# A shortened opening, one product for the spread rows, earlier evictions and a gather that comes out turned

## The reference

```python
h = concat(meta, x_prompt)                      # 272 rows, and 8 samples beside them
u = rmsnorm(h, norm_mix) @ w_in                 # 1024 -> 4640 columns
xc = silu(causal_conv(xa)); q, k = xc @ w_q, xc @ w_k; v = xa @ w_v      # per head, 128 x 128
h_a = mlstm_chunk_scan(q, k, v, ig, fg)         # states C (128 x 128 per head and sample), n, m
y   = ssd_chunk_scan(silu(causal_conv(xbc)), dt, A)
h = h + concat(gated h_a, gated y) @ w_out
xn = rmsnorm(h, norm_ffn)                       # meta rows dropped: 256 + 8 tokens
group = top1(xn @ w_r1); experts = top2(xn @ w_r2 in that group)
h = h + sum_e gate_e * (silu(xn @ w_gate[e]) * (xn @ w_up[e])) @ w_down[e]
return rmsnorm(h, norm_final), the prompt's states, the samples' states
```

## Time and profile before

| | us |
|---|---|
| runs (three) | 786.55, 788.24, 788.31; median 788.24 |
| the profiled execution | 787.24, its span 785.4 |
| PE busy | 752.2 (96%) |
| DVE, ACT busy | 276.8 (35%), 219.8 (28%) |
| bytes moved | 263.68 MB, mean 336 GB/s |

### The profile page before, as it was taken

One profiled execution on the slowest core, in us unless ns is written; L12 is line 12 of the kernel. 1 busy time (PEld: TensorE's weight loads), 2 busy tenths in 40 slices (PEclk: granted clock), 3 DMA queues, 4 the chain that ended last, 5 costly groups with the idle time before them and its releaser, 6 DMA issues.

```text
span 785.4 us, 9604 instructions
## 1 busy us (share of the span) xinstructions
PE 752.2 (96%) x3789; PEld 403.0 (51%) x3789; DVE 276.8 (35%) x657; ACT 219.8 (28%) x630; POOL 30.1 (4%) x89
## 2 busy tenths in 40 slices
PE   6997999998999999999999999999999999999995
PEld 5876888876788887533333333333333333332232
DVE  4934565768877311430030131121210201311204
ACT  4226666738765101611100101001011011001003
POOL 6100000001000100000000000000000000000000
PEclk9999999999999999999999999999999999999998
DMA  9954377965895687779999999999999999999992
GB/s 259 326 187 127 117 227 235 319 217 168 278 310 178 260 331 311 283 275 431 426 428 429 426 427 426 428 426 427 428 425 428 427 426 428 424 428 427 426 399 79
DMA packets 76347, 263.68 MB, mean 336 GB/s; under 512 B 7382, under 2 KB 46554, under 8 KB 62840
## 3 DMA queue, kind: packets, MB, share of 16 engines
q1 hardware_dynamic: 74512, 259.02, 84.4%
q0 software_dynamic: 1568, 3.91, 1.4%
q10 hardware_dynamic: 216, 0.07, 0.0%
HBM read 251.15 MB, written 11.99 MB: 335 GB/s over the span
## 4 chain that ended last, share of the span: by engine, by line
PE 81%; DMA 6%; DVE 6%; ACT 4%; issue 1%; POOL 1%; DVEq 0%; POOLq 0%; ACTq 0%
PE bank L2331 26%; PE bank L2410 12%; PE bank L1908 10%; PE bank L2181 7%; DMA arena<-in_w_down 6%; PE bank L2290 4%; PE bank L1896 4%; PE bank L2356 4%; PE bank L1995 2%; ACT h_tok L1006 1%; DVE h_tok L1442 1%; PE bank L2300 1%; PE bank L2344 1%; DVE xn L1392 1%; PE bank L2309 1%
## 5 line engine op out<-in xcount | busy, mean ns | idle before, releaser
L2331 PE MATMUL bank<-ring,arena 128*64 128x512 f32 x640 | 144.5, 596 | 4.7 <-DMA ring<-in_w_up 2.5
L1908 PE MATMUL bank<-arena,ring 128*128 128x264 f32 (+1 forms) x448 | 109.6, 400 | 4.4 <-ACT xn L928 1.7
L1908 PEld LDWEIGHTS bank<-arena,ring 128*128 128x128 f32 x448 | 84.9, 193 | 21.1 <-issue 2.8
L2331 PEld LDWEIGHTS bank<-ring,arena 128*64 128x64 f32 x640 | 43.5, 137 | 92.6 <-issue 83.1
L513 DVE COPY arena<-bank 64x512 f32<-64x512 f32 x15 | 10.2, 683 | 203.9 <-PE bank L2410 203.9
L2410 PE MATMUL bank<-ring,arena 128*64 128x512 f32 x272 | 60.5, 593 | 1.9 <-DMA ring<-in_w_down 1.9
L1773 DVE TENSOR_TENSOR arena<-bank,WG 128x512 f32<-128x512 f32 x16 | 16.9, 1055 | 126.4 <-PE bank L2331 126.4
L2181 PE MATMUL bank<-arena,ring 128*128 128x264 f32 x256 | 58.4, 387 | 0.0
L2331 PE MATMUL bank<-arena 128*64 128x512 f32 x240 | 54.6, 597 | 0.0
L2181 PEld LDWEIGHTS bank<-arena,ring 128*128 128x128 f32 x256 | 48.3, 190 | 8.5 <-issue 0.3
L1237 ACT ACTIVATE arena<-bank 128x512 f32<-128x512 f32 x15 | 9.0, 597 | 144.7 <-PE bank L2344 144.7
(11 more groups left out here) (401 smaller groups left out, 836.6 us busy)
## 6 DMA issues: line engine op xcount, KB each, us to landing
ring<-in_w_gate SPq DMA_DIRECT2D x20, 2048.0 KB, 26.0
ring<-in_w_up SPq DMA_DIRECT2D x20, 2048.0 KB, 28.5
ring<-in_w_down SPq DMA_DIRECT2D x17, 2048.0 KB, 26.8
ring<-in_w_in SPq DMA_DIRECT2D x9, 2048.0 KB, 10.8
arena<-in_w_down SPq DMA_DIRECT2D x7, 2048.0 KB, 29.4
arena<-in_w_up SPq DMA_DIRECT2D x6, 2048.0 KB, 22.1
arena<-in_w_gate SPq DMA_DIRECT2D x6, 2048.0 KB, 31.8
out<-h_tok SPq DMA_DIRECT2D x16, 512.0 KB, 3.8
```

What stands on the lines that cost most here:

```text
L1908: last = mm(b[:, q0:T], slot_k(UNIT_SLOT[u], 512)[:, k, o:o + P], hT[:, k, q0:T], start=(k == 0), stop=(k == KD - 1))
L2331: last = mm(b[CAP * half:CAP * (half + 1), :], XG[:, k, (e % 2) * CAP:(e % 2 + 1) * CAP], w(kk)[:, half * 512:(half + 1) * 512], start=(k ...
```

## The change

- **Opening.** `ident` is made first on POOL and signals at once; PE starts on extra transposes of `ident` (`turning`, 14, then 8, 6 and 4 between the real ones). ACT's table load stands ahead of its DMA issues. ACT, not DVE, normalises the small tile, and PE transposes the parameters behind tile 0's normalised rows and the second `turning`. POOL's writes of p_m, s_m and xt_dram now come ahead of the router's loads, and so the latter wait for `rows_pre`.
- **Spread rows.** DVE forms RS and RX times a diagonal (RSD, RXD: three multiplications), and PE spreads them with one product of 128 columns and two of 136, in `rows_turned`, which stands behind the seventh tile, ahead of the eighth. `row_exps` moves ahead by one eviction.
- **Evictions.** The samples' values get a signal of their own and are copied by ACT ahead of the wait for `tm_ready`; the first conv tile of head 0 is evicted ahead of `decay_state(1)`.
- **Gather.** xn is the stationary operand and PX moves with 128 columns, so the result is turned already; `rows_out`, `turn` and GT go. It stands at the head of the loop for expert 2p-1.
- **End.** The gain products go ahead, behind expert 15's first projection, into banks 0 and 1; `last_down` uses banks 2 and 3; the third tile of `last_scatter(0)` (8 rows) moves behind `last_down(1)`. DVE's order there is as it was.

```diff
+            link(g.memset(ident[:], 0.0))
+            g.affine_select(out=ident[:], in_=ident[:], compare_op=ALU.not_equal, fill=1.0, base=0, ...).then_inc(s.consts, 1)
...
+            turning(14, 7)
             for i in range(2):
                 pe.wait_ge(x_in[i], 16)
...
+                if i == 0:
+                    turning(8, 7)
...
+            turning(6, 7)
+            pe.wait_ge(s.xn_ready, 2)
             pe.wait_ge(s.params_in, 16 * 8)
...
-            normalised(2, NB + META)
+            dve.wait_ge(s.h_std, 3)
+            v.reciprocal(st3[0:NB + META, 6:7], st3[0:NB + META, 6:7]).then_inc(s.pv_ready, 1)
...
+            def rows_turned():
+                pe.wait_ge(s.rows_exp, 2)
...
+                mm(bank[5][:, 0:HA * 16], ones[0:HA, :], RSD, start=True, stop=True)
+                for j in range(2):
+                    mm(bank[5][j * HD:(j + 1) * HD, P:P + KD * 17], ones[0:HB, 0:HD], RXD[j], start=True, stop=True)
...
+                if n0_ == 6:
+                    rows_turned()
...
-            for h in range(HA):
-                mm(bank[5][:, h * 16:(h + 1) * 16], col(ident[0:HA, :], h), RS[:, :], start=True, stop=True)
-            for c in range(KD):
-                for j in range(2):
-                    last = mm(bank[5][j * HD:(j + 1) * HD, 128 + c * 17:128 + (c + 1) * 17], ...)
...
+                    if h == 0:
+                        evac(HA + XBC_A[h])
                     decay_state(h + 1)
-                    evac(HA + XBC_A[h])
...
-                def gather(p, half, tiles, done=False):
+                def gather(p, half, tiles, first_tile, last_tile):
+                    b, c0 = bank[(6 if p == 0 else 0) + half], p % 4 * P
+                    for k in range(4):
+                        for i in tiles:
+                            last = mm(b[:, k * P:(k + 1) * P], xn[:, i, (4 * half + k) * P:(4 * half + k + 1) * P], PX[:, i, c0:c0 + P], ...)
...
-                turn(0, 0)
...
                     if x_ % 2 == 1 and p < NX // 2:
-                        turn(p, 0)
-                        turn(p, 1)
+                        pe.wait_ge(s.p_ready, r * 4 + (1 + p // 2))
+                        gather(p, 0, range(2), 0, None)
+                        gather_samples(p)
+                        gather(p, 1, range(2), None, 1)
...
-                        last_scatter(0)
+                        last_scatter(0, range(2))
                 last.then_inc(s.d_ps, 1)
-                last_scatter(1)
+                last_scatter(0, range(2, 3))
+                last_scatter(1, range(3))
```

More of the change, by code:

```diff
@@ L330, in program @@
         ARG = carve(arena, 15304, 2, BLKW)
+        RSD = ARG[0:HA, 0, 0:HA * 16]
+        RXD = [ARG[0:HB, 1, j * KD * 17:(j + 1) * KD * 17] for j in range(2)]
         SQT = carve(arena, 15304 + 2 * BLKW, NP - META)
@@ L574, in _ @@
             sp.wait_ge(s.xn_ready, 3)
[L575 removed]
+            sp.wait_ge(s.ht_ps, 10)
             for n in range(3):
@@ L913, in _ @@
                     last.then_inc(s.ht_ready, 1)
+            a.preload_act_table(ACT.Exp)
             act.wait_ge(s.x_abs, 1)
@@ L1406, in _ @@
             conv_taps(1)
+            dve.wait_ge(s.rows_exp, 1)
+            v.tensor_tensor(RSD.rearrange("p (h x) -> p h x", x=16), RS[:, :].unsqueeze(1).to_broadcast([HA, HA, 16]),
+                            bc_last(ident[0:HA, 0:HA], 16), ALU.mult)
+            for j in range(2):
+                last = v.tensor_tensor(RXD[j].rearrange("p (c x) -> p c x", x=17), RX[:, :].unsqueeze(1).to_broadcast([HB, KD, 17]),
+                                       bc_last(ident[0:HB, j:HB:2], 17), ALU.mult)
+            last.then_inc(s.rows_exp, 1)
             conv_gate(0)
@@ L1856, in chunks, with turning @@
                 return last
+            def turning(n, b):
+                for _ in range(n):
+                    tr(bank[b][:, 0:P], ident[:, :], ident[:, :])
+            turning(14, 7)
             for i in range(2):
@@ L2326, in project @@
                     for kk in range(4):
-                        if kk == 2 and between:
-                            between()
                         k = 4 * u + kk
@@ L2366, in one_round @@
                 rows_normed(1)
-                gather(0, 0, range(2))
+                gather(0, 0, range(2), 0, None)
                 rows_normed(2)
@@ L2370, in one_round @@
                 rows_normed(3)
-                gather(0, 1, range(1))
-                turn(0, 0)
+                gather(0, 1, range(1), None, None)
                 rows_normed(4)
-                gather(0, 1, range(1, 2), done=True)
-                project(0, 0, 0, between=lambda: turn(0, 1))
+                gather(0, 1, range(1, 2), None, 1)
+                project(0, 0, 0)
                 project(0, 0, 1)
@@ L2400, in one_round @@
                     if x_ == NX - 2:
+                        pe.wait_ge(s.x_again, 16 * 2)
+                        for c in range(2):
+                            mm(bank[c][:, :], ones[FROW:FROW + 1, :], NFROW[:, c * 512:(c + 1) * 512], start=True, stop=True)\
+                                .then_inc(s.gbc_ps, 1)
                         project(x_ + 1, 1, 0)
@@ L2444, in last_scatter @@
                            start=True, stop=True).then_inc(s.sc_out_ps, 1)
-                pe.wait_ge(s.x_again, 16 * 2)
-                for c in range(2):
-                    mm(bank[2 + c][:, :], ones[FROW:FROW + 1, :], NFROW[:, c * 512:(c + 1) * 512], start=True, stop=True)\
-                        .then_inc(s.gbc_ps, 1)
                 pe.wait_ge(s.ht_sb, r * NX + NX)
```

160 lines of the change are left out of this document (69 added, 91 removed).

## The result

The changed kernel takes 789.77 us (median of 19 runs, 787.27 to 792.95), the kernel before 788.10 (19 runs, 785.25 to 790.48): ratio 1.0023, 95% interval 1.0012 to 1.0034, so 0.9 to 2.7 us slower. Forecast was a median of 786.3. The profiled execution of the changed kernel has a span of 786.7, 1.3 above that of before.

The account below looks back on a forecast made before the run. The experts' weight stream was taken as the bound, its start set by the refill at 340.51. Opening 0.4, head 0 1.9, gather 1.2, less 1.6 at the end: 1.9 earlier, median 786.3 us, range 781.6 to 789.8.

Parts of the forecast that it names:

- the gather's start: Pair 0's gather after opening and head 0: forecast 2.3 us earlier, 0.4 of it from the opening.
- the gather: Gather of pair 0, up to the first projection: 1.2 us earlier, between 0.5 later and 1.5 earlier.
- the stream: Experts' weights from SP's first refill on: fixed bytes at a fixed rate, so work saved in pairs 1 to 7 counts nothing.
- the end: Behind the last weights: 1.6 us later, between 2.6 earlier and 2.7 later; DVE's order 0.9, the clock 0.7.
- head 0: Spread rows and head 0, to the second conv tile: 1.9 us earlier beside the opening, between 0 and 6.
- gate columns: Opening: their start, 13.46 before, was expected near 13.0, 0.4 us earlier, between 0.4 later and 0.8 earlier.
- The gather's lower bound: Gather of pair 0: at 0.14 per instruction, 48 take 6.7 us and it is 0.5 later.
- 1: Rival: gain ahead of the experts is lost on the way, leaving only gather and end; 788.6 us, chance 0.15.
- 2: Rival, head 0: samples' rows come early, their write passing the loads ahead; tile 6.4 earlier, 782.2 us, chance 0.13.
- 3: Rival: TensorE at half clock in `rows_turned`, head 0 and the end; 2.8 later, 791.0 us, chance 0.12.
- 4: Rival, opening: transposes don't raise the clock, gate columns start about 3.1 later; 789.8 us, chance 0.03.
- 5: Rival: work saved in the experts counts, the stream isn't the bound; 7 us more, 779.3 us, chance 0.05.

Follow-up runs that it names:

- e2: Changed kernel with POOL's DMAs in the order of the kernel before: median 786.43 us, ratio to the kernel before 0.9971.
- e14: Kernel before with the change's opening, spread rows and evictions, but POOL's DMAs in the order of before: median 783.93 us, ratio 0.9943.
- e13: Kernel before with the change's opening, spread rows, evictions and POOL order, gather and end as before: median 786.02 us, ratio 0.9970.
- e3: Changed kernel with 12 extra PE products in head 0's idle ahead of the first state read: median 786.81 us, ratio to before 0.9982.
- e1: Changed kernel with the third tile's scatter back beside the other two, gain products left as changed: median 785.13 us, ratio to before 0.9946.
- e9: Changed kernel with 22 extra transposes in PE's idle ahead of the last six instructions: median 787.11 us, ratio to before 0.9994.
- e8: e7 with unit U_B + 1 loaded behind the first two broadcast loads of the samples' values: median 775.04 us, ratio to before 0.9838.
- e6: Changed kernel with one more 512-column PE product in each of pairs 1 to 7: median 788.37 us, ratio to before 0.9999.
- e5: Changed kernel with DVE's and ACT's copies of the last down projection's second half moved ahead: median 785.24 us, ratio to before 0.9964.
- e10: Changed kernel with only e8's SP move of unit U_B + 1: median 780.40 us, ratio to before 0.9901.
- e12: Kernel before with only the change's end (gain products ahead, third tile's scatter moved back): median 790.10 us, ratio 1.0027.
- e7: Changed kernel with both e1's scatter and e2's POOL order: median 781.87 us, ratio to before 0.9917.
- e11: Kernel before with only e8's SP move of unit U_B + 1: median 787.68 us, ratio 1.0001.
- e4: Kernel before with only the change's turned gather, all 8 pairs: median 788.13 us, ratio 0.9997.

## Why the prediction was wrong

The profiled pair gives the sum by the prediction's own terms: 0.64 earlier at the gather's start (forecast 2.3), 1.02 by the gather (1.2), 0.57 later along the stream (nothing), 2.38 later at the end (1.6). That is 1.3 later instead of 1.9 earlier: of the 3.2 between them 1.7 are lost ahead of the gather, 0.8 at the end, 0.6 along the stream and 0.2 in the gather.

- **Failed step, head 0.** "POOL's DMAs move behind `rows_pre`, to a time when POOL and the queues have nothing due before head 0; if they ran into the load at 49.24 they would delay it by under 1 us". No row stood behind the "under 1 us", and nothing due before head 0 holds only near 40 to 42, when POOL gets to them. But POOL idles 8.6 us between the two router loads (6.11 in the profile of before, which could have been read), and that puts the second load and all behind it at 50.8 to 55, beside the 2 MB and the rows. The rows landed 3.1 us later than forecast, and e2 gives 2.4 of that back (e14 against e13 2.2, and 2.1 us of time). The rest of the step held: from the read to the end of the tile 8.9 us were taken, 8.8 forecast, with one fall of the clock in it, which e3 prices at 2.2.
- **Mis-sized term, the end.** By DVE's order the last six instructions were to start 0.9 later; counted from the last weights it was 0.95 (17.23 against 16.28). The clock was put at 0.7, and is 1.4 to 2.65. The bound had 1.8, what a conv tile loses; six instructions of 2.94 us at half the clock could lose up to 2.9. "DVE's spacing hides some", the reason for taking 0.7, did not come: in the executions with 5.59 an instruction of PE takes 0.93 us, longer than the 0.67 of one of DVE's adds. The term's other half, the gain products' 1.9, came as forecast (e1).
- **Right**: gate columns (13.17; though the mean of 12 profiles with this opening is 13.4, of 4 with the old one 13.6, so 0.2 earlier), clock at full behind `rows_turned`, the load at 51.08, the idle of 6.9, the gather's 1.0, the DMA share of 1.0 with PE's waits for weights from 609 on instead of 719, and PE's idle of 3.4 at the end with DVE's copy as releaser. With the extra transposes PE came to speed, as forecast against the Trainium skill's "TensorE: Matmul & The Clock Gate", "Part 4: PE-mode transpose": the first 14 took 3.25 us, 0.23 each, later ones 0.13. That this was the clock is read from the durations alone, since the granted clock reads 1.00 in all stretches of the opening, before and after; the row that shows transposes holding the clock is e9's. The gather's lower bound was mis-added: 48 instructions of 0.14 are 6.7 us against 5.9 before, 0.8 later and not 0.5. They took 5.05.
- **Rivals.** 1: in the profiled pair the gain wasn't lost on the way, it was never made. 2: false here, though e8 shows what it describes: the write waited behind the loads (9.23 us), and once these loads go elsewhere the tile ends at 69.1. 3: true at one of its three places, the end. 4: false, the gate columns started at 13.17. 5: e6 excludes it.
- **What stays open.** The parts timed alone give 2.4 faster, 0.3 faster and 2.1 slower, 0.6 faster together, where the whole is 1.8 slower. With 1.4 to 1.5 us of uncertainty on each the two agree within their intervals, but only just; whether the parts disturb each other by a microsecond wasn't settled. One sign speaks against it: the seven kernels whose times were expected from the change's 789.8 (e1, e2, e3, e5, e6, e9, e10) came out 0.7 to 2.6 us below that, even e6, whose added work was to cost nothing. e6 is 0.9999 of the kernel before (0.9980 to 1.0018), the change 1.0023, and the change itself was not run again beside them. So gains over the changed kernel by two ratios are good to some 2 us.
- **What one profile is worth.** With the change's head and gather as they are the refill came at 338.85, 340.79 (e1), 340.23 (e5), 341.70 (e6) and 341.39 (e9), a spread of 2.9; with those of before at 340.51 and 340.92 (e12). So the 1.66 earlier of the pair is the best of five, and their mean, 340.6, is no gain over these two. Two causes can be seen. The gate columns start anywhere from 13.07 to 13.95 with this opening. And in the Mamba heads the granted clock falls to 0.50 for some 3 us in every profile, in ten of them only at a place that lies near 190 (near 180 in e8), in six near 215 (e5, e6, e9, e12; near 208 in e10; e7 has both falls). In the ten 251.1 to 252.1 us pass from the second conv tile to the gather, in the six 253.0 to 253.5. e12 has the head of before, so the place of the fall isn't the change's doing; what decides it is open, and how often it falls late in runs that weren't profiled isn't known.

## What to carry to other kernels

When a DMA is moved, list what every queue has under way at the time when it really runs, not when its engine gets to it, and count small packets by the time they take from others, not by their bytes. An edit that makes an intermediate result early is worth little until the transfer that carries it stands ahead of large loads that nobody waits for yet: here the state's read came 1.2 us earlier without that (e2) and 6.4 with it (e8). Before a small piece of work is moved behind a large one, read who waits for the small one in program order: eight rows cost 4 us here.

## What the runs showed of the hardware

- The same code at the same place meets the clock differently in different executions. The second conv tile of head 0 took 5.73 us in two profiles without the change's head (before, e11) and 4.04 in two others (e4, e12); one fall of the clock in the Mamba heads lay near 190 in ten profiles and near 215 in six; an idle of 3.38 at the end was followed by six instructions of 4.34 to 4.50 in three profiles and 5.59 in three, and never by 2.94. So a price of the clock that is read from one row can be one of several.
- The six instructions of the end took 1.9 times as long where nearly all of them ran at 1.2 GHz, 1.5 times where the clock came back midway. After an idle of 1.22 (e5), or of 0.83 behind 22 transposes (e9), they ran at full clock.
- Transfers with a DMA share of 1.0 moved 427 GB/s as weights of the experts, and 221 with POOL's small transfers among a weight unit (56 to 58 of the changed kernel).
